# Small columns of a fused two-layer transformer kernel: one shared buffer split into buffers of their own, with a spacer, and a scratch row added

## The chip, the cores and the metric

The kernel runs on one core of one Trainium2 chip. The metric is the device time in microseconds of one execution; the median of three runs of the kernel before is 2111.81 us (2106.22 to 2112.70). Everything below is float32; the matrix products run on TensorE (PE in the profile), the element-wise work on VectorE (DVE), ScalarE (ACT) and GpSimd (POOL), and nearly all transfers are issued by SyncE (SP).

## The reference

Two layers over 512 latent tokens and 256 context tokens, width 1024. Layer 0 mixes tokens with a chunked gMLP, layer 1 with bidirectional retention in 4 heads; both are followed by a squared-ReLU MLP of width 4096. What matters here are the places where small per-token or per-head numbers come in:

```
for i in range(2):
    sh1, s1, g1, sh2, s2, g2 = split(silu(c) @ ada_w[i] + ada_b[i], 6)
    h = x * (1 + s1) + sh1
    y = gmlp(h) if i == 0 else retention(h, ctx, decay)
    x = layernorm(alpha * x + g1 * y) ; x = layernorm(alpha * x + g2 * relu(h2 @ w1)**2 @ w2)

layernorm: (x - mean) * (var + eps) ** -0.5           # one number per token
retention: log_gamma = log1p(-exp(decay))             # 2 directions x 4 heads
           decay_in  = exp(log_gamma[h] * (i - j))    # one scale per head and direction
           headnorm of each head's output: the same (var + eps) ** -0.5
```

The context stream goes through layer 0 too, and feeds the states of layer 1.

## The kernel before, in words

Each weight matrix is cut into 256 units of 128 x 1024 numbers (512 KB). SP loads a unit into one of four `raw` slots; ACT rounds it to float32r (`w_hi`, L855), DVE takes the remainder (`w_lo`, L1125), and each product of two matrices is three matmuls on PE: high by high, high by low, low by high (L554 to L556). The work is in stages: the modulation vectors and the first hidden state (`v0`), the v half of the gMLP (`v`), the gMLP itself (`gmlp`), a layer norm (`ln0a`), MLP (`ffn0`), norm (`ln0b`), retention over four heads (`heads`), norm (`ln1a`), MLP (`ffn1`), norm (`ln1b`). The order on each engine is written out by hand, and engines are held together by counting semaphores alone; no scheduler moves anything, and no dependency hangs on which buffer a number lies in.

Buffers lie in each of SBUF's 128 partitions one after the other in the order in which the code asks for them, each starting at a multiple of 32 bytes; buffers of layer 0 and of layer 1 use the same space again. The change touches the small ones at the end of those that live for the whole kernel:

- `tiny`, 8 numbers per partition. Columns 0 and 1 are `lgh`, the log of gamma of the current head (written by DVE at L1486, read by ACT as the scale of two exponentials at L1054). Column 2 is `mhalf`, the constant -0.5 (set once by POOL at L1649). Columns 4 to 7 are `nbias`, minus mean times rstd of up to four token tiles (written by DVE at L1197, read by ACT at L895).
- `veps` and `rstd`, 8 numbers each: the variance plus epsilon (DVE, L1186) and its power -0.5. The power is taken by POOL in `power` (L1595), one column of one token tile at a time, with the exponent as second operand: 58 such instructions. In a layer norm they stand in POOL's queue between the additions of the last product to the residual (L1605).
- `lg`, 5 rows of 8 numbers: the decay parameters come in by DMA into row 0, and DVE and ACT work out the log of gamma in six short DVE and two ACT instructions at the very start (L1302 to L1313); the result overwrites row 0.

Behind these lie all buffers of the two layers: of layer 0 the residual and gate of the context, the slots `mod0` of the modulation weights, the activations `act_hi0`, `act_lo0`, the gMLP's `wsT`, `rowsum`, `bs`, `bv`, `vtok`, then `mod1` and the norm's gain and shift `lnbc0`; of layer 1 `pa_hi`, `pa_lo`, `v_hi` to `k_lo`, `scr`, `gs`, `y`, `dec`, `rope`, `lnbc1`. In front of them, so not moved by the change, lie `hT_hi`, `hT_lo`, `raw`, `w_hi`, `w_lo`, `res_lat`, `gate_lat`, `stage`, `rbuf`, `gy` and the columns.

Of the kernel before, what the change touches and what calls it, by code (L numbers as in the profile page):

```python
# [28 lines left out]
ALU = mybir.AluOpType  # L29

P = 128
# [180 lines left out]
def build(nc, w_units, mod0_units, mod1_units, xT_d, x_d, ctx_d, cols_d, cvec_d, wsT_d, bs_d, bv_d, ln_d, decay_d, dist_d, rope_d,  # L212
          small_d, out_d):
    keep = ExitStack()
    with keep:
        def sem(name):
            return keep.enter_context(nc.semaphore(name))

        def sb(name, shape, dt=F32, scope=keep):
            return scope.enter_context(nc.sbuf_tensor(name, shape, dt))  # L220
# [27 lines left out]
        mv = sb("mv", [P, 8, 2])  # L248
        veps = sb("veps", [P, 8])
        rstd = sb("rstd", [P, 8])  # L250
        tiny = sb("tiny", [P, 8])
        lgh, mhalf, nbias = tiny[:, 0:2], tiny[:, 2:3], tiny[:, 4:8]
        lg = sb("lg", [P, 5, 8])
        ADAB, LNC, BU, LNG, LNB = 0, 96, 160, 176, 192

        layer0 = ExitStack()
# [81 lines left out]
        rstd_ready = sem("rstd_ready")  # L338
# [13 lines left out]
        lg_dve = sem("lg_dve")  # L352
        lg_act = sem("lg_act")
        pool_const = sem("pool_const")
# [755 lines left out]
        def _(dve):  # L1110
            tt = nc.vector.tensor_tensor
# [195 lines left out]
            dve.wait_ge(lg_dve, 3)  # L1307
            nc.vector.reciprocal(lg[:, 4, :], lg[:, 4, :]).then_inc(lg_dve, 1)
            dve.wait_ge(lg_dve, 4)
            tt(lg[:, 0, :], lg[:, 4, :], lg[:, 1, :], ALU.mult).then_inc(lg_dve, 1)  # L1310
            dve.wait_ge(lg_dve, 5)
            dve.wait_ge(lg_act, 2)
            tt(lg[:, 0, :], lg[:, 0, :], lg[:, 3, :], ALU.mult).then_inc(lg_dve, 1)  # L1313

            dve.wait_ge(const_in, N_CONST)
            def split_mods(g):
# [151 lines left out]
            def head(h):  # L1468
                def rotate(r, a, b, scale, j, at_q):
# [13 lines left out]
                    st = stage_slot("heads", h, j + 1, TOKL)  # L1483
                    tt(st, rbuf[:, 0, :], rbuf[:, 1, :], ALU.add).then_inc(stage_full, 1)

                nc.vector.tensor_copy(lgh[:, :].unsqueeze(2), lg[:, 0, :].rearrange("p (w h) -> p w h", w=2)  # L1486
                                      [:, :, bass.ds(h, 1)]).then_inc(lgh_ready, 1)
                split_lo("heads", h, 2)
                split_lo("heads", h, 3)
# [85 lines left out]
            with nc.vector.Fori(0, HEADS - 1) as h:  # L1575
                head(h)
            head(HEADS - 1)
            ln_split("ln1a", LAT, "ffn1")
            dve.wait_ge(act_drain, before("A", "ffn1"))
# [6 lines left out]
        def _(pool):  # L1586
            gt = nc.gpsimd.tensor_tensor

            def power(phase, i, n, s):

                done = BASE_STAT[phase] + n + 1
                if not isinstance(i, int) or i:
                    done = i * 8 + done
                pool.wait_ge(var_ready, done)
                gt(rstd[:, s:s + 1], veps[:, s:s + 1], mhalf, ALU.pow).then_inc(rstd_ready, 1)  # L1595

            def add_one(phase, i, half, t, tiles):

# [13 lines left out]
            def add_last(phase, i, tiles, ln_phase, between=lambda: None):  # L1612

                for t in range(tiles):
                    add_one(phase, i, 0, t, tiles)
                between()
                for t in range(tiles):
                    add_one(phase, i, 1, t, tiles)
                    if t >= 1:
                        power(ln_phase, 0, t - 1, t - 1)  # L1620
                power(ln_phase, 0, tiles - 1, tiles - 1)
# [24 lines left out]

            nc.gpsimd.memset(scT[:, :, :], 0.0).then_inc(sc_zero, 1)
            nc.gpsimd.memset(ones[:, :], 1.0).then_inc(pool_const, 1)
            nc.gpsimd.memset(mhalf, -0.5).then_inc(pool_const, 1)  # L1649
            pool.wait_ge(res_in, 32)  # L1650
            for t in range(TILES0):
                nc.gpsimd.tensor_scalar(res(t), res(t), ALPHA, None, ALU.mult).then_inc(res_base, 1)
# [8 lines left out]
            for t in range(TILES0):  # L1661
                power("v", 0, t, t)
# [118 lines left out]
```

## Time and profile before

| | |
|---|---|
| median of three runs | 2111.81 us (2106.22, 2111.81, 2112.70) |
| the profiled execution: its time | 2112.70 us |
| its span, first to last instruction | 2110.9 us |
| mean granted TensorE clock | 0.987 of full speed |
| instructions | 27839 |
| busy: PE, DVE, ACT, POOL | 97%, 49%, 28%, 24% of the span |

The profile is of one execution. Its page gives the busy time of each engine, the chain of work that ended last (followed back from the last instruction), and groups of instructions with their mean duration and the idle time before them. Idle time of an engine that is not the bottleneck costs nothing. The trace behind it can be asked for one line, one buffer or one stretch of time.

### The profile page before, as it was taken

What the parts mean: (1) busy time and instruction counts of PE and PEld (TensorE: products, weight loads), DVE (VectorE), ACT (ScalarE), POOL (GpSimd) and SP (SyncE); (2) the same over time, 40 slices, a digit from 0 to 9 for tenths busy, and PEclk for the clock granted to TensorE, in tenths of its full rate; (3) what the DMA queues carried; (4) which work ended last, traced back from release to release, by engine and by line L of the source; (5) the groups of instructions that cost most, each with busy time, mean ns of one, the idle gap of its engine ahead of it and who ended that gap; (6) DMA issues with size and microseconds to landing.
All of it is one profiled execution on the core that took longest, in us unless ns stands there. A gap on an engine that the chain in (4) does not pass through costs nothing.

```text
span 2110.9 us, 27839 instructions
## 1 busy us (share of the span) xinstructions
PE 2049.1 (97%) x9932; PEld 1719.5 (81%) x9932; DVE 1044.0 (49%) x1527; ACT 598.9 (28%) x856; POOL 506.9 (24%) x381
## 2 busy tenths in 40 slices
PE   6999999999999999999999999999999989999996
PEld 3778899888888888888878878878878867888884
DVE  3335554559443344334573553544553576445446
ACT  2222222225212222222244223223313342332221
POOL 0300202337430233023350020020020037223323
PEclk8999999999999999999999999999999999999998
DMA  9642111123223322333121121121221212222321
GB/s 372 264 166 70 60 60 59 62 100 110 87 93 119 119 82 96 119 119 112 57 82 65 49 96 60 60 86 56 75 76 60 70 61 90 98 91 99 119 91 58
DMA packets 58045, 204.32 MB, mean 97 GB/s; under 512 B 6640, under 2 KB 7024, under 8 KB 57840
## 3 DMA queue, kind: packets, MB, share of 16 engines
q1 hardware_dynamic: 57104, 199.96, 27.4%
q10 hardware_dynamic: 864, 3.28, 0.4%
q8 instruction: 55, 0.90, 0.2%
q14 instruction: 22, 0.18, 0.0%
HBM read 201.12 MB, written 2.10 MB: 96 GB/s over the span
## 4 chain that ended last, share of the span: by engine, by line
PE 88%; issue 6%; POOL 2%; DVE 2%; ACT 1%; DMA 1%; SPq 0%; DVEq 0%; POOLq 0%; ACTq 0%
PE bank L554 28%; PE bank L556 28%; PE bank L555 28%; PE bank L664 2%; POOL res_lat L1605 2%; PE bank L750 1%; DVE w_lo L1125 1%; DMA mod<-mod_units_d 1%; POOL res_ctx L1605 0%; DVE bst L1177 0%; PE bank L807 0%; ACT w_hi L855 0%; DVE gy L1232 0%; POOL rstd L1595 0%; DVE res_lat L1287 0%
## 5 line engine op out<-in xcount | busy, mean ns | idle before, releaser
L1125 DVE TENSOR_TENSOR w_lo<-raw,w_hi 128x1024 fp32r<-128x1024 f32 x256 | 342.5, 1338 | 441.1 <-ACT w_hi L855 440.3
L855 ACT ACTIVATE w_hi<-raw 128x1024 fp32r<-128x1024 f32 x256 | 270.3, 1056 | 742.4 <-PE bank L556 741.8
L1605 POOL TENSOR_TENSOR res_lat<-res_lat,gy 128x512 f32<-128x512 f32 x192 | 264.1, 1408 | 869.8 <-DVE gy L1232 860.4
L554 PE MATMUL bank<-hT_hi,w_hi 128*128 128x384 f32 (+2 forms) x1216 | 433.6, 357 | 14.5 <-DVE w_lo L1125 10.2
L555 PE MATMUL bank<-hT_lo,w_hi 128*128 128x384 f32 (+2 forms) x1216 | 428.4, 352 | 0.0
L556 PE MATMUL bank<-hT_hi,w_lo 128*128 128x384 f32 (+2 forms) x1216 | 428.2, 352 | 0.0
L554 PEld LDWEIGHTS bank<-hT_hi,w_hi 128*128 128x128 f32 x1216 | 230.8, 190 | 48.5 <-issue 14.8
L554 PE MATMUL bank<-w_hi,hT_hi 128*128 128x512 f32 x640 | 252.9, 395 | 4.1 <-DVE hT_lo L1134 4.1
L555 PE MATMUL bank<-w_lo,hT_hi 128*128 128x512 f32 x640 | 250.7, 392 | 0.0
L556 PE MATMUL bank<-w_hi,hT_lo 128*128 128x512 f32 x640 | 250.4, 391 | 0.0
L555 PEld LDWEIGHTS bank<-hT_lo,w_hi 128*128 128x128 f32 x1216 | 230.9, 190 | 16.2 <-issue 0.2
L556 PEld LDWEIGHTS bank<-hT_hi,w_lo 128*128 128x128 f32 x1216 | 230.7, 190 | 15.9
L554 PE MATMUL bank<-w_hi,act_hi 128*128 128x512 f32 x576 | 225.6, 392 | 0.0
L556 PE MATMUL bank<-w_hi,act_lo 128*128 128x512 f32 x576 | 224.5, 390 | 0.0
L555 PE MATMUL bank<-w_lo,act_hi 128*128 128x512 f32 x576 | 224.4, 390 | 0.0
L1442 DVE TENSOR_TENSOR stage<-rbuf 128x384 f32<-128x384 f32 (+1 forms) x96 | 67.3, 703 | 231.2 <-ACT rbuf L1011 231.2
L1232 DVE TENSOR_TENSOR gy<-bank,gate_lat 128x512 f32<-128x512 f32 x192 | 129.8, 689 | 100.6 <-POOL res_lat L1605 61.4
L1595 POOL TENSOR_TENSOR rstd<-veps,tiny 128x1 f32<-128x1 f32 x58 | 34.6, 597 | 520.2 <-DVE veps L1186 520.2
L554 PEld LDWEIGHTS bank<-w_hi,hT_hi 128*128 128x128 f32 x640 | 120.8, 189 | 40.5 <-issue 15.0
L554 PE MATMUL bank<-w_hi,pa_hi 128*128 128x512 f32 x384 | 151.3, 394 | 0.5 <-issue 0.2
L556 PE MATMUL bank<-w_hi,pa_lo 128*128 128x512 f32 x384 | 149.8, 390 | 0.0
L555 PE MATMUL bank<-w_lo,pa_hi 128*128 128x512 f32 x384 | 149.7, 390 | 0.0
(150 smaller groups left out, 2427.0 us busy)
## 6 DMA issues: line engine op xcount, KB each, us to landing
raw<-w_units_d SPq DMA_DIRECT2D x256, 512.0 KB, 3.3
mod<-mod_units_d SPq DMA_DIRECT2D x48, 512.0 KB, 8.1
mod<-mod_units_d SPq DMA_DIRECT2D x64, 384.0 KB, 3.8
lnbc<-ln_d SPq DMA_DIRECT2D x8, 512.0 KB, 5.2
xT<-xT_d SPq DMA_DIRECT2D x4, 768.0 KB, 14.0
dec<-dist_d ACTq DMA_DIRECT2D x4, 768.0 KB, 4.4
res_lat<-x_d SPq DMA_DIRECT2D x1, 2048.0 KB, 14.2
out_d<-res_lat SPq DMA_DIRECT2D x4, 512.0 KB, 3.2
```

The source lines that it names most:

```text
L554: nc.tensor.matmul(out, s_hi, m_hi, start=first, stop=False)
L555: nc.tensor.matmul(out, s_hi, m_lo, start=False, stop=False)
L556: return nc.tensor.matmul(out, s_lo, m_hi, start=False, stop=last)
L664: last = nc.tensor.matmul(bank[rows][tile:tile + 32, 0:w], scT[:, n, :], buf[:, s, block * w:(block + 1) * w], start=n < 2, stop=n >= KC - ...
L750: last = nc.tensor.matmul(bank[4 + h][:, j * P:(j + 1) * P], vtok[:, 3 * h + j, col], wsT[:, g, :], start=True, stop=True)
L855: nc.scalar.activation(w_hi[:, slot(phase, k), :], raw[:, s, :], ACT.Copy).then_inc(hi_done, 1)
L1125: tt(w_lo[:, w, :], raw[:, s, :], f32(w_hi[:, w, :]), ALU.subtract).then_inc(lo_done, 1)
L1232: tt(gy[:, e % 2, :], bank[t][:, :], gate_of(t)[:, half * 512:(half + 1) * 512], ALU.mult)\
L1442: tt(st, r, r, ALU.mult).then_inc(stage_full, 1)
L1595: gt(rstd[:, s:s + 1], veps[:, s:s + 1], mhalf, ALU.pow).then_inc(rstd_ready, 1)
L1605: gt(r, r, gy[:, e % 2, :], ALU.add).then_inc(res_added, 1)
```

## The change

The three residents of `tiny` become buffers of their own: `nbias` (8 numbers), `mhalf` (8), `lgh` (2). `lg` gets a sixth row, and a buffer `pad_line` that nothing reads or writes is put behind. The result of the log of gamma goes into row 5 of `lg` and no longer over row 0, so the copy for a head reads row 5. All 8 columns of `mhalf` are set to -0.5, and `power` takes the exponent from the column that has the number of the tile.

Before, `tiny` and `lg` take 32 + 160 = 192 bytes per partition. After, the five take 32 + 32 + 192 + 32 (for 8 used) + 32 = 320. So every buffer behind them starts 128 bytes later. Counting from the start of a partition, the buffers of the layers stood 128 bytes behind a multiple of 256 bytes, all but `lnbc0`, which stood on one; after, they all stand on a multiple of 256, and `lnbc0` 128 bytes behind one. The list of instructions on each engine, their order, their sizes and their semaphores are the same, apart from the names in them and the size of one memset (128x8 for 128x1).

```diff
-        tiny = sb("tiny", [P, 8])
-        lgh, mhalf, nbias = tiny[:, 0:2], tiny[:, 2:3], tiny[:, 4:8]
-        lg = sb("lg", [P, 5, 8])
+        nbias = sb("nbias", [P, 8])
+        mhalf = sb("mhalf", [P, 8])
+        lg = sb("lg", [P, 6, 8])
+        lgh = sb("lgh", [P, 2])
+        sb("pad_line", [P, 8])
...
-            tt(lg[:, 0, :], lg[:, 4, :], lg[:, 1, :], ALU.mult).then_inc(lg_dve, 1)
+            tt(lg[:, 5, :], lg[:, 4, :], lg[:, 1, :], ALU.mult).then_inc(lg_dve, 1)
             dve.wait_ge(lg_dve, 5)
             dve.wait_ge(lg_act, 2)
-            tt(lg[:, 0, :], lg[:, 0, :], lg[:, 3, :], ALU.mult).then_inc(lg_dve, 1)
+            tt(lg[:, 5, :], lg[:, 5, :], lg[:, 3, :], ALU.mult).then_inc(lg_dve, 1)
...
-                nc.vector.tensor_copy(lgh[:, :].unsqueeze(2), lg[:, 0, :].rearrange("p (w h) -> p w h", w=2)
+                nc.vector.tensor_copy(lgh[:, :].unsqueeze(2), lg[:, 5, :].rearrange("p (w h) -> p w h", w=2)
                                       [:, :, bass.ds(h, 1)]).then_inc(lgh_ready, 1)
...
-                gt(rstd[:, s:s + 1], veps[:, s:s + 1], mhalf, ALU.pow).then_inc(rstd_ready, 1)
+                gt(rstd[:, s:s + 1], veps[:, s:s + 1], mhalf[:, s:s + 1], ALU.pow).then_inc(rstd_ready, 1)
...
-            nc.gpsimd.memset(mhalf, -0.5).then_inc(pool_const, 1)
+            nc.gpsimd.memset(mhalf[:, :], -0.5).then_inc(pool_const, 1)
```

## Rows read from the trace of the kernel before

**Rows 1.** The page, part 1: busy us, share of the span, instructions.
```profile
PE 2049.1 (97%) x9932; PEld 1719.5 (81%) x9932; DVE 1044.0 (49%) x1527; ACT 598.9 (28%) x856; POOL 506.9 (24%) x381
```

**Rows 2.** The page, part 4: the chain that ended last, by engine.
```profile
PE 88%; issue 6%; POOL 2%; DVE 2%; ACT 1%; DMA 1%; SPq 0%; DVEq 0%; POOLq 0%; ACTq 0%
```

**Rows 3.** Start of DVE and POOL in order: start us, us, instruction, [idle before].
```profile
12.02 0.17 DVE L1313 TENSOR_TENSOR lg<-lg 128x8 f32<-128x8 f32 x1 [0.57 <-ACT lg L934]
22.78 1.23 DVE L1125 TENSOR_TENSOR w_lo<-raw,w_hi 128x1024 fp32r<-128x1024 f32 x1 [10.59 <-ACT w_hi L855]
...
0.98 0.20 POOL L1648 MEMSET ones<- 128x128 f32 x1
1.13 0.10 POOL L1649 MEMSET tiny<- 128x1 f32 x1
...
86.08 11.66 POOL L1652 TENSOR_SCALAR res_lat<-res_lat 128x1024 f32<-128x1024 f32 x4 [84.86 <-DMA res_ctx<-ctx_d]
```

**Rows 4.** Instructions on tile tiny: duration ns min/median/max, first and last start.
```profile
L1595 POOL TENSOR_TENSOR rstd<-veps,tiny x58: 543/548/1520, 188.3 to 2095.2; 128x1 f32<-128x1 f32 x58
L1197 DVE TENSOR_SCALAR tiny<-mv,rstd x10: 196/198/201, 473.6 to 1727.0; 128x1 f32<-128x1 f32 x10
L895 ACT ACTIVATE res_lat<-res_lat,tiny,rstd x10: 1240/1241/1247, 473.9 to 1727.3; 128x1024 f32<-128x1024 f32 x10
L1054 ACT ACTIVATE dec<-dec,tiny x8: 918/922/937, 1120.1 to 1619.9; 128x768 f32<-128x768 f32 x8
L1486 DVE COPY tiny<-lg x4: 163/1228/1239, 1073.6 to 1562.4; 128x2 f32 x3, 128x2 f32<-128x2 f32 x1
```

**Rows 5.** The chain's steps on L1595, first and last: start us, us.
```profile
472.72 0.50 POOL rstd L1595
480.99 1.06 POOL rstd L1595
...
1729.21 1.06 POOL rstd L1595
```

**Rows 6.** The chain from 0 to 36 us: start us, us, what.
```profile
7.91 11.48 DMA mod<-mod_units_d
...
31.56 0.43 PE bank L554
...
34.08 0.23 PE bank L555
```

**Rows 7.** The scaling of lnbc by ACT, lnbc0 twice, then lnbc1.
```profile
L888 ACT ACTIVATE lnbc<-lnbc x1: 1902/1902/1902, 469.0 to 469.0; 128x2048 f32<-128x2048 f32 x1
L888 ACT ACTIVATE lnbc<-lnbc x1: 1905/1905/1905, 1046.2 to 1046.2; 128x2048 f32<-128x2048 f32 x1
L888 ACT ACTIVATE lnbc<-lnbc x1: 1899/1899/1899, 1720.7 to 1720.7; 128x2048 f32<-128x2048 f32 x1
```

**Rows 8.** Landing of the four pairs of lnbc loads, at 443, 972, 1701, 1975 us.
```profile
DMA to landing us min/median/max: 4.3/5.1/5.8
...
DMA to landing us min/median/max: 4.9/5.4/6.0
...
DMA to landing us min/median/max: 4.1/4.6/5.0
...
DMA to landing us min/median/max: 5.4/5.8/6.2
```

**Rows 9.** Groups by line and form: xcount, busy us, mean ns, idle before.
```profile
L554 PE MATMUL bank<-w_hi,hT_hi 128*128 128x512 f32 x640 | 252.9, 395 | 4.1 <-DVE hT_lo L1134 4.1
L554 PE MATMUL bank<-w_hi,act_hi 128*128 128x512 f32 x576 | 225.6, 392 | 0.0
L556 PE MATMUL bank<-w_hi,act_lo 128*128 128x512 f32 x576 | 224.5, 390 | 0.0
L554 PE MATMUL bank<-w_hi,pa_hi 128*128 128x512 f32 x384 | 151.3, 394 | 0.5 <-issue 0.2
L554 PE MATMUL bank<-v_hi,pa_hi 128*128 128x512 f32 x144 | 56.5, 392 | 0.0
```

**Rows 10.** Stretches: us, busy us (count) of PE, PEld, DVE, ACT, POOL, then PEclk, DMA share, GB/s.
```profile
20.00:34.00 14.00, 9.20 (x25) 5.81 (x22) 9.60 (x21) 6.57 (x11) 0.00 (x0) 0.52 1.02 411
...
1736.00:1744.00 8.00, 6.50 (x16) 5.16 (x17) 7.06 (x15) 5.40 (x13) 2.52 (x2) 0.57 0.00 1
```

## The prediction

> **What bounds the kernel now.** I read the shares of busy time first, and the reader should see one engine that hardly rests: PE is busy for 2049.1 of 2110.9 us, DVE for half, POOL for a quarter of the span [rows 1]. The chain that ended last says the same from the other side: 88% of it is PE, 2% each POOL and DVE, 1% ACT [rows 2]. So a change to what DVE, ACT or POOL do counts only in the few places where PE waits for them (the layer norms and the first 34 us), and in the rest only what makes the matmuls themselves longer or shorter. I then asked for every instruction that touches the split buffer [rows 4], for the places where one of them is a step of the chain [rows 5], and last for anything in this trace that tells whether an address 128 bytes further on is faster or slower, since that is the one thing that the change does to the large buffers [rows 7 to 9].
>
> **Part 1: the start (the memset, the log of gamma).** The memset of the exponent grows from 1 to 8 columns. It took 0.10 us with 1 column, and the one before it, with 128 columns, 0.20 us [rows 3]: so at most 0.10 us more, at 1.1 us, in front of a POOL that then stands idle for 84.86 us [rows 3]. Cost 0. The log of gamma is the same six DVE instructions with another destination row. The last starts at 12.02 us and takes 0.17, and DVE then waits 10.59 us for the first weights [rows 3]; were all six ten times as slow (some 9 us more), they would still be just done in that gap. Cost 0.
>
> **Part 2: the exponent (L1595).** 58 powers, median 548 ns, both operands a single column [rows 4]. After the change the second operand lies in another buffer and moves with the tile number; the instruction is otherwise the same. Eight of them are steps of the chain, five in the first norm of layer 0 and three in the first norm of layer 1: six of 0.50 to 0.56 us and two of 1.06 [rows 5]. Most of the others lie behind matmuls that do not wait for them. I expect 0 per power. The trace has no row with the operand elsewhere, so I bound it: upwards each of the six could become as long as the two that took 1.06, 6 x 0.55 = +3.3 us; downwards each of the eight could lose 0.4 us and come to the time of the smallest things POOL does (the 0.10 us memset), -3.2 us. I take 0, because the 58 already sit at 543 to 548 ns from minimum to median although their first operand and their result change column from one to the next: which column is read makes no difference of more than some ns there.
>
> **Part 3: the bias column and the head's scale.** Ten DVE instructions write `nbias` (196 to 201 ns) and ten ACT ones read it (1240 to 1247) [rows 4]. Before, the four columns lie in one buffer with `mhalf` and `lgh`; after, in one with nothing else. The spread over ten is 5 and 7 ns. If it all vanished, or came twice, that would be about 10 x 12 ns = 0.1 us. The copy that writes `lgh` runs four times, at 163 to 1239 ns, and the eight exponentials that use it take 918 to 937 ns [rows 4]; the copy is issued when DVE has next to nothing else due, and the exponentials come 46 us or more after the first copy (1120.1 against 1073.6). Cost 0.
>
> **Part 4: all buffers of the layers stand 128 bytes further on.** This is the part with the reach, since most of the time goes through them. Three groups of rows speak to it.
>
> ACT scales `lnbc0` twice and `lnbc1` once, the same 2048 columns. Before the change `lnbc0` starts on a multiple of 256 bytes and `lnbc1` 128 bytes off one, so these three rows compare the two placements: 1902 and 1905 ns against 1899 [rows 7]. The difference is at most 6 ns in 1900, 0.3%. Cost 0.
>
> For PE the rows are weaker. The operands `hT` (not moved) and `act`, `pa`, `v` (moved) all stand 128 bytes off a multiple of 256 now, and their matmuls take 390 to 395 ns alike [rows 9]. That shows that the buffer does not matter, not that the placement doesn't. In the layout after, `act` and `pa` are on a multiple of 256 while `hT` stays. I take 0, by ACT's rows as the nearest of an engine reading the same lanes, and keep 0.3% of the matmuls that read moved buffers as bound on both sides. Matmuls on `act` are 3 x 576, on `pa` 3 x 384 with weights and 3 x 144 with `v` [rows 9], 3312 in all, and one follows the other every 0.23 us at full clock [rows 6], 762 us. 0.3% of it is 2.3 us.
>
> For transfers there is one stretch where they bound the time: the chain hangs for 11.48 us on the modulation weights at the start [rows 6], which land in `mod0`, a moved buffer. The loads of `lnbc` are again the comparison. On a multiple of 256 the first of a pair landed after 4.3 and 4.9 us and the second after 5.8 and 6.0; 128 bytes off, 4.1 and 5.4, and 5.0 and 6.2 [rows 8]. The means are 4.60 against 4.75 and 5.90 against 5.60, so -3% and +5%, and the scatter within one placement is larger than either. On 11.48 us that is -0.4 to +0.6 us. I take 0.
>
> A rule of the notes bears on the same place. The Trainium skill (page "DMA: Bandwidth & Descriptors", section "How a descriptor splits into AXI transactions") says that a descriptor which does not start on a multiple of 256 bytes is served by a first transaction from the boundary below, whose unused bytes still cost. By that rule a 4096-byte row of `mod0` is 17 transactions now and 16 after, or 132 and 128 beats of 32 bytes; an estimate by that page is 3 to 6% off the 11.48 us, a gain of 0.35 to 0.7 us. The trace does not agree visibly, since the `lnbc` loads show no order by placement [rows 8]; and its gain would be too small to see in the whole.
>
> **The sum.** 0 + 0 + 0 + 0. The profiled execution has a span of 2110.9 us and a time of 2112.7, 1.8 us around it; I expect the same of the kernel after. That run was the highest of three, and the median is 2111.81. I predict 2111.5 us, between span and median, as a spread of 6.5 us towards the low side has been seen. A time that moved by less than 0.3% (6.3 us) is what a measurement of this kernel can't tell from no change.
>
> **The rivals.**
>
> *The placement slows the matmuls.* If a moving operand on a multiple of 256 bytes were read more slowly, the price would be on 3312 matmuls or 762 us: 1% of it is +7.6 us, 2119 us. It becomes visible from 6.3 / 762 = 0.83%, 1.9 ns in a step of 230. For it: no PE row shows such an operand. Against it: the three ACT rows, which differ between the placements by 6 ns in 1900 at most [rows 7]. This is the case on the slower side. It could also go the other way by the same size.
>
> *The powers change.* +3.3 us or -3.2 us from part 2, so 2115 or 2108 us. For it: the second operand is the only thing an instruction of the chain reads from another place. Against it: the flat 543 to 548 ns.
>
> *The first 34 us come out otherwise.* PE runs at half clock (1.2 GHz, of 2.4) from 20 to 34 us, where it has waited for data: granted clock 0.52 [rows 10], and steps of 0.43 instead of 0.23 us [rows 6]. The same after the wait of the second norm, 0.57 from 1736 to 1744 us [rows 10]. Eleven matmuls in the first stretch at 0.20 us more each are 2.2 us. Should transfers into `mod0` land some tenths of a us sooner or later, PE's wait changes, and with it perhaps how long the low clock lasts: with the page's transfers (-0.7) and one such stretch gone (-2.2) the time would be 2108.6; with both stretches gone, 2.2 + 14 x 0.20 = 5.0 us, 2106. This is how I read the 2106.22 among the three runs, without a row for it.
>
> *The change does more than it says.* Splitting a buffer would free engines of each other if a dependency hung on the buffer; here only semaphores order them, and they are unchanged. I give this nothing of its own.
>
> **How the numbers follow.** No change that can be told: 0.88. In that are the powers' case (0.04) and the start's (0.06), which by their price stay within 0.3%. The matmuls slower by 0.83% or more: 0.04. Faster by more than 0.3%, from the matmuls the other way or from the start with both low-clock stretches shorter and transfers sooner: 0.06. Of scatter of the measurement beyond 0.3% another 0.02 goes to the slower side, as three runs of one kernel spread over 6.5 us. So faster 0.06, same 0.88, slower 0.06. The range: downwards the powers (-3.2) and the start at its bound (-0.4), with the lowest run of before at 2106.2, give 2106 and a little; upwards the powers (+3.3), the start (+0.6) and part of the 2.3 us of the matmuls from 2111.5 give 2116. 2105.8 to 2116.
>
> **What would show it.** The powers at L1595 (two lines lower after) at 543 to 548 ns again; `nbias` at 198 and its readers at 1241 ns; the scaling of `lnbc` at 1899 to 1905 ns with `lnbc0` and `lnbc1` having changed placement; matmuls on `act` and `pa` at 390 to 394 ns; the step on the modulation weights at about 11.5 us. Wrong would be: matmuls on `act` and `pa` that moved by 2 ns or more while those on `hT` did not, powers above 600 ns in the median, or a first stretch of low clock that is absent or twice as long.

## The result: 0.66% slower, and the profile after

The kernel after takes 2125.11 us (median of four runs, 2122.37 to 2125.77) against 2111.88 (four runs, 2106.22 to 2112.70). The ratio is 1.0066, 95% interval [1.0046, 1.0086]. It is not the quotient of the two medians, which is 1.0063; the same holds for the ratios further down, where each quotient lies inside its interval. The time lies outside the range that was given (2105.8 to 2116.0), and on the side that had a chance of 0.06. The profiled execution took 2127.02 us, its span is 2125.2.

The first part of its page; each entry is the busy time in us, the share of the span and the number of instructions:

```profile
span 2125.2 us, 27839 instructions
PE 2063.8 (97%) x9932; PEld 1719.1 (81%) x9932; DVE 1049.8 (49%) x1527; ACT 599.2 (28%) x856; POOL 497.7 (23%) x381
```

Beside [rows 1], PE is busy 14.7 us longer with the same 9932 matmuls, and the span is 14.3 us longer. ACT has not changed, POOL is 9 us less busy and DVE 6 us more. So PE's pauses together did not grow (61.8 us before, 61.4 after): the matmuls themselves take longer. The groups by line and form say which. The columns are the count, busy us and mean ns of one; the first name behind the arrow is the moving operand, the second the stationary one, whose 128 columns are loaded as weights:

```profile
L556 PE MATMUL bank<-w_hi,hT_hi 128*128 128x512 f32 x640 | 252.4, 394 | 4.6 <-DVE hT_lo L1136 4.6
L556 PE MATMUL bank<-w_hi,act_hi 128*128 128x512 f32 x576 | 228.4, 396 | 0.0
L558 PE MATMUL bank<-w_hi,act_lo 128*128 128x512 f32 x576 | 227.4, 395 | 0.0
L557 PE MATMUL bank<-w_lo,act_hi 128*128 128x512 f32 x576 | 227.3, 395 | 0.0
L556 PE MATMUL bank<-w_hi,pa_hi 128*128 128x512 f32 x384 | 153.1, 399 | 0.5 <-issue 0.2
L556 PE MATMUL bank<-v_hi,pa_hi 128*128 128x512 f32 x144 | 56.5, 392 | 0.0
```

Against [rows 9], `act` with `w` went from 390-392 to 395-396 ns and `pa` with `w` from 394 to 399, while `hT` with `w` (395, now 394) and `pa` with `v` (392) stayed. These durations overlap their neighbours, so what one matmul costs is its step, from its own start to the start of the next. I took the mean of the steps from the start times in the trace (steps under 300 ns, so without the pauses):

| moving, stationary | matmuls | step before, ns | step after, ns |
|---|---|---|---|
| w, act | 1728 | 226.9 | 232.7 |
| w, pa | 1152 | 227.1 | 232.7 |
| w, hT | 1920 | 227.1 | 227.2 |
| v, pa | 432 | 227.1 | 227.3 |
| hT, w (mostly 384 columns) | 3648 | 188.7 | 188.9 |

Two groups are slower by 5.6 to 5.8 ns, 2.5%, and 2880 x 5.7 ns is 16 us. The sum of all steps of a group says the same: `act` from 393.2 to 403.2 us, `pa` with `w` from 273.8 to 279.6, together +15.8 us. The span grew by 14.3, so the rest of the kernel gave 1.5 us back.

A reader can see it on the chain without any statistics. Each trip of the first MLP's loop has its modulation matmuls on it, and the distance from the first such row of one trip to the first of the next is one trip (start us, us, what). Before:

```profile
567.70 1.41 PE bank L664 x12
...
638.28 1.42 PE bank L664 x12
```

and after:

```profile
570.87 1.42 PE bank L666 x12
...
642.34 1.42 PE bank L666 x12
```

70.58 us became 71.47, 0.89 us more, and there are 144 matmuls of `w` with `act` in a trip: 144 x 5.8 ns = 0.84 us.

What the change was written about, the small columns, behaves as forecast. Instructions on the exponent's buffer, in the form of [rows 4]:

```profile
L1597 POOL TENSOR_TENSOR rstd<-veps,mhalf x58: 537/548/1519, 187.6 to 2109.5; 128x1 f32<-128x1 f32 x58
L1651 POOL MEMSET mhalf<- x1: 104/104/104, 1.1 to 1.1; 128x8 f32 x1
```

and on the bias and the head's scale:

```profile
L1199 DVE TENSOR_SCALAR nbias<-mv,rstd x10: 195/196/198, 475.9 to 1738.1; 128x1 f32<-128x1 f32 x10
L897 ACT ACTIVATE res_lat<-res_lat,nbias,rstd x10: 1239/1242/1246, 476.1 to 1738.3; 128x1024 f32<-128x1024 f32 x10
...
L1056 ACT ACTIVATE dec<-dec,lgh x8: 919/921/938, 1129.8 to 1630.6; 128x768 f32<-128x768 f32 x8
L1488 DVE COPY lgh<-lg x4: 163/1229/1233, 1082.1 to 1571.4; 128x2 f32 x3, 128x2 f32<-128x2 f32 x1
```

All medians are within 2 ns of before.

### The profile page after: what moved, and what is told of

Its sections match the earlier page's. It is cut to its first block, busy times and chain, and to the rows that moved or that the text cites. A ratio compares the mean times of both kernels' runs of the same rounds, so it can differ in the third digit from the quotient of the medians.

```text
span 2125.2 us, 27839 instructions
## 1 busy us (share of the span) xinstructions
PE 2063.8 (97%) x9932; PEld 1719.1 (81%) x9932; DVE 1049.8 (49%) x1527; ACT 599.2 (28%) x856; POOL 497.7 (23%) x381
## 4 chain that ended last, share of the span: by engine, by line
PE 93%; issue 2%; DVE 2%; POOL 2%; DMA 1%; ACT 0%; SPq 0%; DVEq 0%; POOLq 0%; ACTq 0%
PE bank L556 30%; PE bank L558 29%; PE bank L557 29%; PE bank L666 2%; PE bank L752 1%; POOL res_lat L1607 1%; DMA mod<-mod_units_d 1%; DVE w_lo L1127 1%; POOL rstd L1597 0%; PE bank L809 0%; PE bank L703 0%; ACT w_hi L857 0%; PE bank L676 0%; DVE res_lat L1289 0%; DVE bst L1179 0%
## 5 line engine op out<-in xcount | busy, mean ns | idle before, releaser
L1127 DVE TENSOR_TENSOR w_lo<-raw,w_hi 128x1024 fp32r<-128x1024 f32 x256 | 349.9, 1367 | 453.0 <-ACT w_hi L857 452.2
L556 PE MATMUL bank<-hT_hi,w_hi 128*128 128x384 f32 (+2 forms) x1216 | 432.4, 356 | 13.5 <-DVE w_lo L1127 9.1
L557 PE MATMUL bank<-hT_lo,w_hi 128*128 128x384 f32 (+2 forms) x1216 | 427.2, 351 | 0.0
L556 PEld LDWEIGHTS bank<-hT_hi,w_hi 128*128 128x128 f32 x1216 | 230.4, 189 | 47.0 <-issue 14.8
L556 PE MATMUL bank<-w_hi,hT_hi 128*128 128x512 f32 x640 | 252.4, 394 | 4.6 <-DVE hT_lo L1136 4.6
L557 PE MATMUL bank<-w_lo,hT_hi 128*128 128x512 f32 x640 | 250.1, 391 | 0.0
L557 PEld LDWEIGHTS bank<-hT_lo,w_hi 128*128 128x128 f32 x1216 | 230.5, 190 | 16.3 <-issue 0.2
L558 PEld LDWEIGHTS bank<-hT_hi,w_lo 128*128 128x128 f32 x1216 | 230.3, 189 | 15.9
L556 PE MATMUL bank<-w_hi,act_hi 128*128 128x512 f32 x576 | 228.4, 396 | 0.0
L558 PE MATMUL bank<-w_hi,act_lo 128*128 128x512 f32 x576 | 227.4, 395 | 0.0
L557 PE MATMUL bank<-w_lo,act_hi 128*128 128x512 f32 x576 | 227.3, 395 | 0.0
L1597 POOL TENSOR_TENSOR rstd<-veps,mhalf 128x1 f32<-128x1 f32 x58 | 34.6, 597 | 522.5 <-DVE veps L1188 522.5
L556 PEld LDWEIGHTS bank<-w_hi,hT_hi 128*128 128x128 f32 x640 | 120.6, 188 | 40.9 <-issue 15.3
L556 PE MATMUL bank<-w_hi,pa_hi 128*128 128x512 f32 x384 | 153.1, 399 | 0.5 <-issue 0.2
L557 PE MATMUL bank<-w_lo,pa_hi 128*128 128x512 f32 x384 | 151.6, 395 | 0.0
```

Of the source, the lines that this page charges most:

```text
L556: nc.tensor.matmul(out, s_hi, m_hi, start=first, stop=False)
L557: nc.tensor.matmul(out, s_hi, m_lo, start=False, stop=False)
L558: return nc.tensor.matmul(out, s_lo, m_hi, start=False, stop=last)
L1127: tt(w_lo[:, w, :], raw[:, s, :], f32(w_hi[:, w, :]), ALU.subtract).then_inc(lo_done, 1)
L1597: gt(rstd[:, s:s + 1], veps[:, s:s + 1], mhalf[:, s:s + 1], ALU.pow).then_inc(rstd_ready, 1)
```

## The experiments

The theory, called R below: a matmul steps slower where its two operands start differently towards multiples of 256 bytes. Before, `w`, `hT`, `act` and `pa` all start 128 bytes behind such a multiple; after, `act` and `pa` start on one and `w` does not. `v` moved together with `pa`, and `hT` stayed with `w`. The rivals: S, that the split of the small columns costs; A, that any move of the layers' buffers costs; P, that the place of the stationary operand alone decides.

### e1 and e2: the placement without the split, and the split without the placement

e1 is the kernel before with one line more:

```diff
         lg = sb("lg", [P, 5, 8])
+        sb("spare", [P, 32])
```

> The kernel before with one unused buffer of 128 bytes behind lg; the small columns stay together. Theory R (a matmul steps slower where its two operands stand differently towards multiples of 256 bytes): the 2880 matmuls with w_hi or w_lo moving and act or pa stationary step at 232.7 ns for 227, so +16 us on PE; in all as the changed kernel, +11 to +16 us (2123 to 2128). Rival S (the split of the small columns costs the time): as before, 2112 within 4 us, and 227 ns everywhere.

Measured: 2125.58 us (five runs) against 2107.40 for the kernel before on the same chip, ratio 1.0071 [1.0047, 1.0095]. Steps of `w` with `act` and `pa` 232.4 to 232.8 ns. The group rows:

```profile
L555 PE MATMUL bank<-w_hi,act_hi 128*128 128x512 f32 x576 | 228.3, 396 | 0.0
L556 PE MATMUL bank<-w_lo,act_hi 128*128 128x512 f32 x576 | 227.3, 395 | 0.0
```

An unused buffer of 128 bytes alone makes the whole loss. S, which gave 2112 within 4 us here, has fallen.

e2 is the changed kernel with a larger spacer:

```diff
-        sb("pad_line", [P, 8])
+        sb("pad_line", [P, 40])
```

> The changed kernel with its spacer 128 bytes larger, so that the buffers of the layers stand 256 bytes behind where they stood before the change. Theory R: all steps at 227 ns, time back at that of the kernel before, 2112 within 4 us. Rival S: 2125, as the changed kernel. Rival A (any move of these buffers costs, since before they happened to stand well): slower than 2116.

Measured: 2110.31 us (ten runs), ratio 1.0008 [0.9997, 1.0019]. Steps 226.8 to 227.4 ns in these groups.

```profile
L556 PE MATMUL bank<-w_hi,act_hi 128*128 128x512 f32 x576 | 225.3, 391 | 0.0
L557 PE MATMUL bank<-w_lo,act_hi 128*128 128x512 f32 x576 | 224.1, 389 | 0.0
```

With the whole split in it and every buffer 256 bytes on, the kernel can't be told from the one before. S has fallen again and A too, and this is the form in which the change costs nothing that can be measured (by the interval at most 0.19%).

### e3 and e4: all buffers moved, or the weights moved against hT

```diff
+        sb("spare", [P, 32])
         hT_hi = sb("hT_hi", [P, KC, TOK0], F32R)
```

> The kernel before with 128 unused bytes ahead of the first large buffer, so that all buffers move together and stand on multiples of 256 bytes. Theory R: the pairs keep their distance, 227 ns in every group, 2112 within 4 us. Rival P (the place of the stationary operand alone decides, on a multiple of 256 bytes it is slow): all 8928 or so matmuls slower by 5.7 ns, about +50 us, 2160. Rival S: 2112.

Measured: 2108.02 us (ten runs), ratio 1.0002 [0.9990, 1.0014]; 227 ns in every group of 512 columns with `w` or `v` moving, and 189 with `hT` moving, as before. With `act`, `pa` and `hT` now on multiples of 256 bytes as stationary operands nothing is slower, so P has fallen too.

In e4 the same line stands ahead of `w_hi`, so that `hT` and `raw` stay.

> The kernel before with 128 unused bytes between raw and w_hi: hT and raw stay, w_hi, w_lo and all behind them move. Theory R: act and pa with w match again (227 ns); the 5568 matmuls of hT with w don't: those of 512 columns (1920 with hT stationary) step at 232.7 for 227, those of 384 columns at about 180 for 174, in all 5568 x 5.7 ns = +32 us, 2144. Rival P: the stationary operands on a multiple of 256 bytes are act, pa and, with hT moving, w: 2880 + 3648 matmuls, +37 us, but none with hT stationary. Rival S: 2112.

Measured: 2130.90 us (four runs), ratio 1.0103 [1.0080, 1.0126]. Now `w` with `hT` steps at 232.5 ns and `w` with `act` is at 227. The first row is of before, the others of e4:

```profile
L556 PE MATMUL bank<-hT_hi,w_lo 128*128 128x384 f32 x768 | 257.4, 335 | 0.0
...
L557 PE MATMUL bank<-hT_hi,w_lo 128*128 128x384 f32 x768 | 259.0, 337 | 0.0
...
L557 PE MATMUL bank<-w_hi,hT_lo 128*128 128x512 f32 x640 | 253.5, 396 | 0.0
...
L557 PE MATMUL bank<-w_hi,act_lo 128*128 128x512 f32 x576 | 224.3, 389 | 0.0
```

The loss has changed place as R says, and P, which wanted nothing slower with `hT` stationary, fails here too. But its size is 23.5 us and not 32, and the time that R expected, 2144, was missed: where `hT` is the moving operand and `w` the stationary one the means rose by 2.8 to 4.0 ns per step and not by 5.7. Why less is open. By steps it is 1920 x 5.4 ns and 3648 x 3.3 ns, 22.4 us.

### e5 to e9: other distances

The `spare` of e1 with other sizes, one run each. The kernel before took 2107.13 us beside e5 and e7 and 2108.96 beside e6 and e9, one run each too. Single runs of one kernel spread over 9 us, so the times rank nothing here; the means over hundreds of steps do.

> As e1, with 64 unused bytes for 128: act and pa stand 64 bytes further on against w than before. Theory R with two classes of 128 bytes each within 256 (which class the start lies in decides): the class of act and pa changes only by moves of 128, and a half move gives something between, some 230 ns for the 2880 matmuls with act or pa, +8 us. Theory R with any distance from a multiple of 256 as bad as another: 232.7 ns, +14 us. If only a multiple of 256 in the distance is good and the loss grows with it, between the two.

> As e1, with 192 unused bytes, that is 64 short of 256. If the pattern is even around a multiple of 256: as e5, to 0.5 ns. If it is a matter of which operand stands ahead (the order in time of weight load and stream): different from e5, and one of the two at or below 227 ns.

> As e1, with 32 unused bytes. The steps of the matmuls with w moving and act or pa stationary so far: 227.0 ns at no distance, 233.3 at 64 bytes (e5c), 232.6 at 128 (e1), 227 to 230 at 192 (e7c). Theory R, with a loss as soon as the stationary operand stands a little further on: 233 ns, time as e5c. If the loss grows from 0 to 64: near 230. I expect 233.

> As e1, with 224 unused bytes, 32 short of 256. Theory R, falling back towards no distance: 227 to 229 ns, time within 5 us of before. If there is a better distance than none, it would be here: below 226 ns in the groups with act and pa; I give that 1 in 10.

| bytes that act and pa are moved against w | us | mean step of w with act or pa, ns |
|---|---|---|
| 0 (before) | 2107.13, 2108.96 | 227.0 |
| 32 (e6) | 2122.91 | 233.3 |
| 64 (e5) | 2122.00 | 233.4 |
| 128 (e1) | 2125.58 | 232.6 |
| 192 (e7) | 2111.64 | 227.1 to 230.3 by group |
| 224 (e9) | 2127.53 | 233.3 |
| 256 (e2) | 2110.31 | 227.0 |

Even 32 bytes cost all of it, and the loss does not grow with the distance. e5 and e6 came out as the case in which any distance is as bad as another. e9 was a miss: I had expected it to fall back towards 227, and it was as slow as the others. No distance was below 227 ns, so none of them gains on the kernel before. Only 192 stands out, with about a third of the loss (229.0 ns on the mean), and the pattern is not even around 256 (64 against 192: 233.4 and 229.0). So e7's first case is out, and its second holds only in part: it is different from e5, but neither of the two is as a whole at or below 227. Why 192 is milder is open, and why 224 is not.

The group at 64 bytes, beside its undisturbed neighbour:

```profile
L557 PE MATMUL bank<-w_hi,hT_lo 128*128 128x512 f32 x640 | 249.9, 390 | 0.0
L555 PE MATMUL bank<-w_hi,act_hi 128*128 128x512 f32 x576 | 228.6, 397 | 0.0
```

On its chain the steps alternate where those of before are even, 225 to 228 ns (start us, us, what):

```profile
554.01 0.24 PE bank L557
554.25 0.23 PE bank L555
554.48 0.24 PE bank L556
554.72 0.23 PE bank L557
554.95 0.24 PE bank L555
555.18 0.23 PE bank L556
```

By start times these are 231 and 236 ns in turn. They follow the turn and not the line: L555, L556 and L557 each have both. The changed kernel alternates more widely in the same stretch, 238 and 229 ns; 232.7 is a mean of such turns. Sorted by token tile, half and chunk, the means at 64 bytes lie between 233.0 and 233.7 ns in the first MLP, so no address within the buffers stands out.

### e8 and e10: one part of a pair moved

If the two reads that meet are the streaming operand and the weights for the next matmul, another step of a triple should be slow than if a matmul suffers from its own pair (a triple is the three matmuls of one product, in the order high by high, high by `w_lo`, low by `w_hi`). e8 moves the low parts of `act` and `pa`:

```diff
+        sb("spare0", [P, 32], scope=layer0)
         act_lo0 = sb("act_lo0", [P, CH, TOK0], F32R, layer0)
...
+        sb("spare1", [P, 32], scope=layer1)
         pa_lo = sb("pa_lo", [P, PW], F32R, layer1)
```

> 128 unused bytes between act_hi and act_lo, and between pa_hi and pa_lo: the high parts stay, the low parts and all behind them move. In each triple of matmuls the order is high by high, high by w_lo, low by w_hi. Theory R-own (a matmul suffers from the distance between the two operands it multiplies): the third of a triple, act_lo or pa_lo with w_hi, 232.7 ns, the first and second 227. Theory R-next (the weights of the next matmul are read while this one streams, and these two reads meet): the second of a triple, which streams w_lo while act_lo or pa_lo is loaded, 232.7 ns, the first and third 227. With v moving and pa stationary: R-own slows the first and second, R-next the first and third. Either way 960 + 288 matmuls by 5.7 ns, +7 us.

Measured: 2122.86 us against 2105.02, one run each, where +7 us was expected; by steps it is 15 us. Steps of the triple with `act`: 226.8, 232.5, 234.1 ns, with `v` and `pa`: 233.0, 232.2, 234.1. Both expectations missed: with `act` the second and the third are slow, with `v` all three. A pairing of both kinds would fit, that a step is slow if the moving operand differs from its own weights or from those loaded meanwhile. The last row is of before, the others of e8:

```profile
L558 PE MATMUL bank<-w_hi,act_lo 128*128 128x512 f32 x576 | 228.6, 397 | 0.0
L557 PE MATMUL bank<-w_lo,act_hi 128*128 128x512 f32 x576 | 228.0, 396 | 0.0
...
L556 PE MATMUL bank<-w_hi,act_hi 128*128 128x512 f32 x576 | 225.2, 391 | 0.0
...
L556 PEld LDWEIGHTS bank<-w_hi,act_hi 128*128 128x128 f32 x576 | 110.5, 192 | 24.8
L557 PEld LDWEIGHTS bank<-w_lo,act_hi 128*128 128x128 f32 x576 | 108.2, 188 | 24.3
...
L554 PEld LDWEIGHTS bank<-w_hi,act_hi 128*128 128x128 f32 x576 | 108.2, 188 | 22.0
```

One weight load also took longer, 192 for 188 ns: the one that runs while the third matmul streams (with `pa` 191). e10 tests the mixed rule with `w_lo` alone moved:

```diff
+        sb("spare0", [P, 32])
         w_lo = sb("w_lo", [P, SPL, UNIT], F32R)
+        sb("spare1", [P, 32])
         res_lat = sb("res_lat", [P, LAT, D])
```

> The kernel before with w_lo alone moved by 128 bytes against everything else (128 unused bytes on each side of it, so all behind it moves by 256). Theory R, own or next (a step is slow if the moving operand differs in class from its own stationary one or from the weights that are loaded meanwhile): with act, pa or hT stationary only the second matmul of a triple, which streams w_lo, 232.5 to 233 ns, the first and third 227. With hT moving and w stationary: the second (its weights are w_hi, but w_lo is loaded meanwhile) and the third (its weights are w_lo) slow, the first not. Rival R-step (a change of class from one load to the next is what costs): with act, pa or hT stationary nothing is slower. Time: 1600 matmuls by 5.7 ns and 2 x 1216 by 3 to 5, +16 to +21 us.

Measured: 2139.71 us against 2108.96, one run each: +30.8 us where +16 to +21 was expected, and the slowest of all; by steps it is 31 us. With `pa` stationary the triple is 228.6, 233.7, 227.2 ns, nearly as the rule says. With `act` it is 235.6, 234.3, 230.0 and with `hT` 231.6, 233.8, 228.5, which it does not. With `hT` moving the means of the triple rose by 2.6, 1.5 and 3.4 ns, where the first was to stay. R-step has fallen, since steps are slower with `act`, `pa` and `hT` stationary, and the mixed rule holds in one group of several. That the same placement gives different triples in `act` and `pa`, and the steady turns at 64 bytes, suggest that a step depends also on how the one before it went; this is argued and not shown.

## Why the prediction was wrong, point by point

**What bounds the kernel** was right: PE, and only what makes its matmuls longer counts. This is what happened.

**Parts 1 to 3** (memset, log of gamma, exponent, bias, head's scale), each put at 0, were right in mechanism and size. The eight powers on the chain take 0.51 to 0.55 and 1.06 us as before, so the bounds of +3.3 and -3.2 us were never approached.

**Part 4** failed, at the sentence that took 0 for PE "by ACT's rows as the nearest of an engine reading the same lanes", with a bound of 0.3%. The measured value is 2.5% per step, 5.7 ns in 227, and some 16 us in all. The rows were rightly called weak: before, no row shows a stationary and a moving operand of the weight products that differ in placement. But I then let an engine with one operand from memory stand for one with two, and bounded the matmuls by its spread of 6 ns in 1900. ACT's rows go on saying what they said: the scaling of `lnbc` takes 1901, 1899 and 1896 ns after, with both placements exchanged. They were true, and no evidence on PE.

The second fault was in what was compared. I asked whether the place of a buffer matters, and e3 shows that it does not. What matters is the place of one operand towards the other. That the change would make such a distance was in my hands from the layout: `hT` and `w` stay, `act` and `pa` move. I also called `act` and `pa` moving operands in the rival, where they are stationary. It counted 3312 matmuls; 432 of them have `v` moving, which moved along, and were spared.

**The rival on the slower side** was the right kind of cause, slower matmuls by placement, with another mechanism: it blamed an operand that stands on a multiple of 256 bytes, and e3 has all of them there and none slower. It named 1.9 ns per step as the point from which it would be seen, and 2119 us for 1%; the step grew by 5.7 ns, three times that point. I gave it 0.04. With no row of the disputed case and 762 us under it, that was far too little, and the range should have held it.

**The start.** I had offered transfers into `mod0` and the length of the low clock. Ten of the twelve profiled kernels have equal steps of `w` with `hT` in the first stage (in e4 and e10 they are slower), and in them the end of it goes with the granted clock between 20 and 34 us. Before the change it is 0.52 [rows 10]; of e5 and then e7:

```profile
20.00:34.00 14.00, 8.79 (x38) 5.44 (x38) 10.45 (x21) 6.56 (x11) 0.00 (x0) 0.76 1.03 412
```

```profile
20.00:34.00 14.00, 8.72 (x39) 5.44 (x38) 10.45 (x21) 6.58 (x11) 0.00 (x0) 0.76 1.02 412
```

At 0.52 to 0.56 (before, e2, e9, e8) the gate products that open the gMLP start on the chain at 184.95 to 185.56 us, at 0.70 to 0.76 (after, e3, e1, e6, e7, e5) at 183.58 to 184.78. So more or less time at 1.2 GHz goes with an end up to 2 us later or sooner, near the 2.2 us that I had worked out; no run changes the clock alone, so that it is the cause is argued. Between before (185.51) and the changed kernel (184.78) it is 0.7 of the 1.5 us that were given back. The other 0.8 us is not traced. The wait on the modulation weights is no part of it that follows placement. Of the changed kernel:

```profile
6.55 11.22 DMA mod<-mod_units_d
```

11.48 us before [rows 6] and 11.22 after, but 11.86 in e1 and 11.77 in e3 with `mod0` equally on a multiple of 256, and 11.77 in e2 with it 128 bytes off. The rule of the Trainium skill on descriptors that start off a multiple of 256 bytes (page "DMA: Bandwidth & Descriptors", section "How a descriptor splits into AXI transactions") would have given 0.35 to 0.7 us there, by the estimate in the prediction; if it acts on these writes, it is below this scatter.

## What to carry to other kernels

When a change moves buffers, look at each matmul's two operands as a pair and ask whether their distance stays; a small buffer put in front of some of them and not of others is such a change, and in this kernel padding to 256 bytes left nothing to measure (ratio 1.0008). A range may only be narrowed by rows of the engine and the number of operands in question: if every row stands on one side of the disputed property, the bound has to come from somewhere that has crossed it, or be left wide.

## What the runs showed that I had not expected

A matmul of 512 columns with `w` moving steps at 227 ns at full clock while the operand pairs start alike towards 256 bytes, and at 232.5 to 233.4 where `act` and `pa` start 32, 64, 128 or 224 bytes further on. 192 bytes cost about a third of that. Moving `w_lo` alone cost more than any other placement tried (up to 235.6 ns in a group of e10). One weight load lasted 192 ns for 188 in e8. What in the reading of the two operands collides is not settled by these runs.

The kernel before spreads from 2103.87 to 2113.32 us over the 20 runs on the first chip of the experiments, and its medians, 2111.88 beside the changed kernel and 2107.40 here, stand 4.5 us apart; so the comparisons above are against runs of before on the same chip.
